# Where the causal mask of the prompt's attention is applied: two instructions on VectorE in place of matmuls with the identity

## What is computed

```
z = einsum('bqhd,bkhd->bhqk', q[:, lo:hi], k[:, :hi]).astype(float32) * scale + b
mask = arange(hi)[None, :] < arange(lo, hi)[:, None]          # strictly causal
log_keep = where(mask, log_sigmoid(-z), 0.0)
remain = cumsum(log_keep, axis=-1, reverse=True)
a = exp(where(mask, z + remain, -inf))
out = einsum('bhqk,bkhd->bqhd', a, v[:, :hi])
```

## Time and profile before

| | us |
|---|---|
| three runs | 1403.56, 1393.55, 1397.66 |
| median | 1397.66 |
| the profiled execution | 1393.66 |
| its span, first to last instruction | 1391.9 |
| busy in that span: PE, DVE, ACT, POOL | 1204.0, 505.8, 272.5, 159.8 |

### The profile page before, as it was taken

The page is one execution under the profiler, slowest core; times in us unless marked ns, Lnnn a source line. Parts: engine busy times, 40 slices in busy tenths (PEclk is TensorE's granted clock), DMA queues, the critical chain, the costliest instruction groups (busy, mean ns, idle before and its releaser), DMA issues.

```text
span 1391.9 us, 22841 instructions
## 1 busy us (share of the span) xinstructions
PE 1204.0 (87%) x9564; PEld 739.9 (53%) x9564; DVE 505.8 (36%) x830; ACT 272.5 (20%) x442; POOL 159.8 (11%) x227
## 2 busy tenths in 40 slices
PE   7999999778899789989959999699888888877882
PEld 4788555456777567777747755343333333332330
DVE  2012466865565865644622343421100110110003
ACT  2122345411221422322310011101000000000000
POOL 4000000122211321111100000101100011001000
PEclk9999999966999789999979999799989999998887
DMA  7114100265877999999999340699999999999985
GB/s 250 61 61 153 53 9 22 105 205 174 267 263 296 361 344 380 365 378 333 377 317 361 125 194 31 229 427 424 426 427 427 427 426 426 424 428 425 428 352 201
DMA packets 103636, 396.08 MB, mean 285 GB/s; under 512 B 14258, under 2 KB 34882, under 8 KB 83056
## 3 DMA queue, kind: packets, MB, share of 16 engines
q1 hardware_dynamic: 84288, 313.42, 57.3%
q0 software_dynamic: 15200, 78.29, 14.9%
q10 hardware_dynamic: 4048, 2.93, 0.6%
HBM read 386.19 MB, written 16.27 MB: 289 GB/s over the span
## 4 chain that ended last, share of the span: by engine, by line
PE 69%; DMA 12%; DVE 9%; issue 6%; ACT 2%; SPq 1%; DVEq 0%; POOLq 0%; ACTq 0%
PE ps L1288 15%; PE ps L1311 6%; PE ps L760 6%; PE ps L763 6%; DMA arena<-in_w_gate_exp 5%; DVE arena L1970 5%; PE ps L1113 4%; DMA arena<-in_cache_v 4%; PE ps L1175 4%; PE ps L1096 4%; PE ps L910 3%; PE ps L944 2%; PE ps L1084 2%; PE ps L831 1%; PE ps L1274 1%
## 5 line engine op out<-in xcount | busy, mean ns | idle before, releaser
L1288 PE MATMUL ps<-arena 128*64 128x512 f32 x512 | 255.5, 658 | 67.4 <-issue 65.9
L1289 PE MATMUL ps<-arena 128*64 128x512 f32 x512 | 256.0, 658 | 0.0
L1288 PEld LDWEIGHTS ps<-arena 128*64 128x64 f32 x512 | 74.7, 152 | 214.5 <-issue 212.2
L1970 DVE STREAM_TRANSPOSE arena<-arena 128x1024 f32<-128x1024 f32 x128 | 149.8, 1216 | 0.1
L617 POOL DMA_INDIRECT arena<-in_cache_k,arena x64 | 67.1, 1048 | 572.6 <-DVE arena L1970 316.1
L1096 PE MATMUL ps<-mixers,arena 128*128 128x272 f32 x512 | 131.1, 404 | 0.0
L910 PE MATMUL ps<-arena 128*32 128x128 f32 x2048 | 83.1, 308 | 37.1 <-DVE arena L1970 25.2
L1096 PEld LDWEIGHTS ps<-mixers,arena 128*128 128x128 f32 x512 | 94.5, 192 | 23.7 <-issue 6.9
L910 PEld LDWEIGHTS ps<-arena 128*32 128x32 f32 x2048 | 64.9, 123 | 47.1 <-DVE arena L1970 34.7
L2217 DVE TENSOR_TENSOR arena<-ps,router_w 128x1024 f32<-128x1024 f32 x16 | 19.6, 1225 | 192.8 <-PE ps L1274 192.7
L763 PE MATMUL ps<-arena,mixers 128*128 128x512 f32 x192 | 87.4, 606 | 1.5 <-DMA arena<-in_w_in 1.5
(11 more groups left out here) (358 smaller groups left out, 1426.2 us busy)
## 6 DMA issues: line engine op xcount, KB each, us to landing
arena<-in_cache_v SPq DMA_DIRECT2D x256, 256.0 KB, 7.3
arena<-in_w_gate_exp SPq DMA_DIRECT2D x32, 2048.0 KB, 32.3
arena<-in_w_up_exp SPq DMA_DIRECT2D x32, 2048.0 KB, 36.8
arena<-in_w_down_exp SPq DMA_DIRECT2D x22, 2048.0 KB, 37.5
mixers<-in_w_down_exp SPq DMA_DIRECT2D x10, 2048.0 KB, 37.3
arena<-in_w_in SPq DMA_DIRECT2D x6, 2048.0 KB
arena<-in_w_in SPq DMA_DIRECT2D x16, 512.0 KB
arena<-expert_outs SPq DMA_DIRECT2D x4, 1024.0 KB, 8.1
```

The costliest lines, as they stand in the source:

```text
L1288: mm(ps[0:BLK, 1 + u, :], own, wgv[w][:, k, :], start=k == 0, stop=k == KD - 1)
L1289: last = mm(ps[BLK:P, 1 + u, :], own, wuv[w][:, k, :], start=k == 0, stop=k == KD - 1)
L1970: v.transpose(out, keys_of(n)[:, 2 * half:2 * half + 2, :].rearrange("p j (b k) -> p j b k", k=32)).then_inc(S("keys_turned"), 1)
```

## The change

PE no longer adds `neg_lt`. The scores of a pair are eight matmuls, one for each block and head. DVE now masks twice. First, between the last sum of the losses and the signal `attn_losses`, it multiplies the four diagonal squares of a_L by `mask_lt`. Second, between the subtraction of the sums and the signal `attn_args`, it adds `neg_lt` to the four diagonal squares of z. Each time one instruction takes the three squares at the columns 0, 512 and 1024 (`diag3`, a strided view with a broadcast mask), and a second takes the square at 896. Two waits on DVE's own chain are added per head in the losses and one in the arguments.

```diff
+        def diag3(v):
+
+            return arena[:, v:v + 1536].rearrange("p (a b) -> p a b", a=3)[:, :, 0:P]
+
+        Z_AT, L_AT = (A0, 2560), (A0 + 2560, A0 + 8960)
...
-                for own in ((0, 1, 2), (3,)):
-                    for s in own:
-                        o = SB_OFF[s]
-                        for e in range(2):
-                            mm(ps[:, 5 * e + o // 512, o % 512:o % 512 + SB_LEN[s]], kT[64 * e:64 * e + 64, p, P * s:P * s + P],
-                               qT[64 * e:64 * e + 64, p, P * s:SEQ], start=True, stop=False)
-                    for s in own:
-                        o = SB_OFF[s]
-                        for e in range(2):
-                            last = mm(ps[:, 5 * e + o // 512, o % 512:o % 512 + P], ident[:, :], neg_lt[:, :],
-                                      start=False, stop=True)
+                for s in range(4):
+                    o = SB_OFF[s]
+                    for e in range(2):
+                        last = mm(ps[:, 5 * e + o // 512, o % 512:o % 512 + SB_LEN[s]], kT[64 * e:64 * e + 64, p, P * s:P * s + P],
+                                  qT[64 * e:64 * e + 64, p, P * s:SEQ], start=True, stop=True)
                 last.then_inc(S("attn_scores"), 1)
...
-                v.tensor_tensor(a_L, a_L, a_t, ALU.add).then_inc(S("attn_losses"), 1)
+                chain(v.tensor_tensor(a_L, a_L, a_t, ALU.add))
+                chain.wait()
+                chain(v.tensor_tensor(diag3(L_AT[e]), diag3(L_AT[e]), over(mask_lt, P, 3, P), ALU.mult))
+                v.tensor_tensor(a_L[:, 896:1024], a_L[:, 896:1024], mask_lt[:, :], ALU.mult).then_inc(S("attn_losses"), 1)
+                chain.wait()
                 dve.wait_ge(S("attn_losses"), h + 1)
...
-                    v.tensor_tensor(attn_z[e], attn_z[e], ps_attn(e), ALU.subtract).then_inc(S("attn_args"), 1)
+                    chain(v.tensor_tensor(attn_z[e], attn_z[e], ps_attn(e), ALU.subtract))
+                    chain.wait()
+                    own = attn_z[e][:, 896:1024]
+                    chain(v.tensor_tensor(diag3(Z_AT[e]), diag3(Z_AT[e]), over(neg_lt, P, 3, P), ALU.add))
+                    v.tensor_tensor(own, own, neg_lt[:, :], ALU.add).then_inc(S("attn_args"), 1)
```

## The result

The changed kernel took 1387.87 us in the median of 20 runs (1384.18 to 1404.79), the kernel before 1397.48 (1390.72 to 1405.74). The ratio is 0.9948, with a 95% interval of 0.9927 to 0.9969, so it is faster by 7.3 us (4.3 to 10.2). The two medians lie 9.6 us apart; I go by the ratio and its interval. The forecast was 1392.2 us, 5.5 us under before. Two more comparisons of the same kernel, e7 on chip 11 and e11 on chip 14, gave 0.9948 (0.9919 to 0.9977) and 0.9924 (0.9895 to 0.9954).

The account below looks back on a forecast made before the run. PE was taken to bound the prompt's attention. Mask matmuls removed, 7.9 us, less three DVE mask waits of 0.79 us, gave 5.5 us: 1397.66 - 5.5 = 1392.2 us, range 1386 to 1401.

Parts of the forecast that it names:

- The mask matmuls: PE in the prompt's attention: removing sixteen per pair saves 1.98 us per pair, 7.9 us in all, all on the path.
- The bracket: Grouped profile view of what the mask matmuls take on PE: 7.7 us by weight loads, 9.3 us by matmuls.
- The masks on the losses and the arguments: New DVE work per head ahead of each of two signals: 0.79 us each, bounds 0.5 and 1.2 us.
- Which of the 16 groups count: Mask groups on the path: pair 0's first losses, last arguments of pairs 1 and 3; 3 x 0.79 us.
- The walk: Step through pairs 0 to 3 with shifted times: PE ahead by 1.19, 2.38, 4.36 after pair 2's scores, finally 5.5 us.
- The pause of pair 0: PE's wait for DVE's first losses in pair 0: 2.3 us where it was 1.5.
- The cover of head 4: Pair 2: head 4's losses come at 215.2 us, PE at 215.3, so PE does not wait; nothing over.
- The stage: Prompt's attention, from first scores to L881: 5.5 us shorter, with bounds of 3.8 and 7.8 us.
- Rival B: Longer PE pauses make the clock fall inside the attention stage: 8.6 us lost, 3.1 us slower, 1400.8 us; chance 7%.
- a clock under 1.00 in the stage: Sign in the changed kernel's attention profile that would show the forecast wrong; no size given.
- Rival A: Gain given back behind the attention stage as the clock falls earlier: 1.9 us left, 1395.8 us, or none, 1397.7; chance 18%.

Follow-up runs that it names:

- e7: The changed kernel run once more, unchanged, on chip 11; 0.9948 of the time of the kernel before.
- e11: The changed kernel run a third time, unchanged, on chip 14; 0.9924 of the time of the kernel before.
- e1: The changed kernel with DVE's masks also removed, so neither engine masks; 0.9974 of the time of the kernel before.
- e2: The kernel before with DVE's masking instructions added, so both engines mask; 0.9997 of the time of the kernel before.
- e3: The changed kernel with the argument masks added before DVE waits for PE's sums; 0.9983 of the time of the kernel before.
- e8: The changed kernel with each of the 16 groups of masks done twice on DVE; 1.0034 of the time of the kernel before.
- e6: The changed kernel with argument masks before DVE's wait and two unused matmuls in PE's pause of pair 0; 0.9933 of the time of the kernel before.
- e4: The changed kernel with five unused matmuls on PE ahead of its wait for pair 0's first losses; 0.9978 of the time of the kernel before.
- e5: The kernel before with 23 unused matmuls on PE ahead of pair 0's scores; 1.0136 of the time of the kernel before.
- e12: e3 run once more, unchanged; 0.9991 of the time of the kernel before.
- e9: e6 with two more unused matmuls in PE's pause before L881; 0.9897 of the time of the kernel before.
- e10: e6 run once more, unchanged; 0.9927 of the time of the kernel before.

## Why the prediction was right, and where it was not

The forecast was a gain of 5.5 us, and 7.3 (4.3 to 10.2) was measured. Step by step:

1. *The mask matmuls, 1.98 us per pair.* All on the path, as said. The size was too small by 0.25 to 0.3 us per pair: 9.0 us for four pairs by e1, and e2 against the changed kernel at full clock (122.0 - 113.0) says the same. I had counted the starts of the mask's own twelve and four. That count ended at the projection's weight load (151.93), and its first matmul starts 0.11 us later (152.04); and the scores themselves, split by the masks, took 2.13 + 0.42 = 2.55 us, where they now take 2.36, 0.19 less. 1.98 + 0.11 + 0.19 = 2.28. The bracket, up to 9.3, held it.
2. *The masks on the losses and the arguments, 0.79 us each.* Measured 0.80. The interpolated 556 ns for 384 elements was 558, and the strided, broadcast form cost nothing extra.
3. *Which of the 16 groups count.* Three, at the forecast places; e2 gives 2.4 us for them. e3 takes two of them off again for 1.5 us (113.0 to 111.5), and e8 brings up heads 3, 4 and 7. The walk had found heads 3 and 4 nearly due; head 7 it had put under what the projections cover, which held at one group's cost and not at two. The pause of pair 0 came out 0.2 us shorter than walked.
4. *The cover of head 4, "just covered".* It was. L831 of head 4 has no wait in the changed kernel, but its weight load waits 0.42 us for DVE's L1819. Before, that load started 0.43 us ahead of the matmul; now it starts 0.24 ahead, at 213.48, and the matmul starts at 213.72, as far behind the projection's first as before (3.54 us).
5. *The stage.* Forecast 5.5 us shorter, measured 5.0 in all three profiles. That is 9.0 - 2.4 - 1.6: two errors that nearly cancel, the matmuls sized too low by 1.1 and the clock left out. That the sum came so near is in part luck.
6. *Rival B* was given 7%, and its mechanism was there in three of three profiles of the changed kernel. The prediction itself had named a clock under 1.00 in the stage as a sign that it was wrong, and that sign came. The price was wrong: I took the 19 us at 0.55 of the earlier trace rows as the length of a fall. Inside the stage the clock returns after 3 to 4 us, and a fall costs 1.5 to 1.7 us and not 8.6. Why it stays low so much longer between 305 and 324 us, where PE is busy for 17 of the 19, is not shown. And that the clock had stood a pause of 2.31 us before L881 was no argument that it would stand one of 2.1 elsewhere.
7. *Rival A*, the pause before L881 growing to 3.1 us with the clock at half behind it, was also seen (0.50 at 260 us). It costs little by itself: L849's matmuls take 3.68 us instead of 2.38. What I did not see is that the clock can cost 10 us more or less in one piece of the cache stage. In e7 it is low there while PE is busy for 21.57 of 22 us, so a low clock does not stand beside an idle PE alone, as my reading of the earlier trace rows had it. The three profiles of the changed kernel, two with the short piece and one with the long, don't show that the change brings it on.

Two things stay open. The first is that the three comparisons of the changed kernel, 7, 7 and 11 us, are together more than its stage's 5.0; the intervals of the first two hold 5.0, that of the third (6.4 to 14.7) doesn't. The second is e3 against e6: the same stage length, and gains of 2.4 and 1.3 us in two comparisons against 9.4 and 10.2 in two others. Three things differ: the filler, and with it the clock in pair 0 in executions that no profile shows; the chips; and how often an execution takes the long form of the cache stage. Against the filler as the whole answer stand e4, which has it and gained 3 us, and e1, whose pause in pair 0 was 1.3 us with the clock at 1.00 and which gained 4 of 9 us; both ran on e3's chip. For the third speaks the kernel before: beside e5 to e8 its 29 executions fall into 15 of 1387.7 to 1394.0 us, with a granted clock of 0.916 in the mean, and 14 of 1398.3 to 1404.0 us with 0.911, and none between. The low clock in the cache stage could be what parts them, but no profile ties the two together. I tried no experiment on that stage itself, and none with e3 and e6 on one chip.

## What to carry to other kernels

Find the places where the pacing engine waits for the engine that gets the new work, and count only the work that stands ahead of those signals: 3 of 16 groups here. What is removed from PE is measured from start to start of what surrounds it, not of what is removed, since its neighbours can get shorter too (0.3 us per pair here). A pause that grows from 1.5 to 2.1 us on PE can also cost the clock for the next 3 to 4 us, as it did here in all three profiles of the changed kernel and in neither of e3's version. Work that does not need the awaited result, like the masks on the arguments, should be done before the wait and not behind it; that made the stage 1.5 us shorter. And where one stage of a kernel varies by 20 us with the same instructions, compare the stage that was changed, and run rival versions side by side on one chip before ranking them.

## What was not expected of the hardware

- The granted clock fell in or just behind pauses of PE of 2.1 to 2.9 us in pair 0 in 4 of 7 profiles (the three of the changed kernel and e8; not in e2, e3 and e12), and in none of the 7 with a pause of 1.5 us or less there. It was back within 3 to 4 us, and the loss was 1.5 to 1.7 us. Unused matmuls in the pause went with a clock of 1.00 in all four profiles that had them (e4, e6, e9, e10), but with the pause open it stayed in three as well. At the pause before L881 it fell behind every one of 2.38 to 3.90 us (ten profiles) and behind none of 2.31 us (before, e1 and e5). The Trainium skill, page "TensorE: Matmul & The Clock Gate", section "Part 1: The HAM clock gate", says that the moment at which the clock rises varies between runs of one kernel. Here it is the fall that varies: at the same pause of 2.1 us the clock falls 0.5 us into L831's matmuls in the first profile of the changed kernel, 1.2 us in e7 and 0.9 us in e11.
- A stage with the same instructions (the cached attention) took from 473.6 to 494.2 us over fourteen profiles, while the experts' stage took 472.5 to 475.9. In one piece of it, from L944's first matmul row to its 257th, PE's clock was at half for 13.7 us in seven profiles and for 34.1 us in six, and the piece took 65.1 and 74.9 us.
